# Down projection of an encoder layer: casts of the second token half's first eight tiles in two portions, and the first weight unit of each output pair taken tile by tile

## The reference, cut to what matters

```
def swiglu(x, w_gate, w_up, w_down):
    return (jax.nn.silu(x @ w_gate) * (x @ w_up)) @ w_down
...
    h = h + FFN_RES * swiglu(rmsnorm(h, ffn1_norm[layer]), ffn1_w_gate[layer], ffn1_w_up[layer], ffn1_w_down[layer])
    h = h + token_mixing(...)
    h = h + FFN_RES * swiglu(rmsnorm(h, ffn2_norm[layer]), ffn2_w_gate[layer], ffn2_w_up[layer], ffn2_w_down[layer])
return rmsnorm(h, final_norm)[:, N_META:]
```

## Time and profile before

| | |
|---|---|
| median of 3 runs | 2661.55 us (2661.48 to 2663.52) |
| profiled execution: its own time, its span | 2661.98 us, 2660.0 us |
| mean granted TensorE clock | 0.968 of full speed |
| busy: PE, DVE, ACT, POOL | 2492.4, 1634.8, 754.2, 126.2 us |
| second phase of the first block | about 613 to 935 us |
| second phase of the second block | about 2317 to 2640 us |

### The profile page before, as it was taken

How to read it: one execution, slowest core, us unless ns; L and a number is a source line. 1 busy time by engine, 2 the same in 40 slices (tenths; PEclk the granted TensorE clock), 3 DMA queues, 4 the chain that set the end, 5 groups by cost and what they waited for, 6 DMA issues and landing times.

```text
span 2660.0 us, 37759 instructions
## 1 busy us (share of the span) xinstructions
PE 2492.4 (94%) x15811; PEld 2375.9 (89%) x15811; DVE 1634.8 (61%) x1967; ACT 754.2 (28%) x1005; POOL 126.2 (5%) x233
## 2 busy tenths in 40 slices
PE   5999999999999999898989878959999999999998
PEld 4899999999999988787877757859999999999998
DVE  6766666665142357877878776386666666643422
ACT  6222222223132322232222323152222222322321
POOL 2000000002010000000000000100000000201000
PEclk8999999999999999999999979989999999999999
DMA  5212212217252311011011211311221222454331
GB/s 201 65 56 78 75 57 77 75 49 289 75 177 96 124 44 32 25 34 37 17 42 34 85 55 40 116 36 62 68 78 62 68 78 67 164 184 129 122 107 62
DMA packets 204581, 222.32 MB, mean 84 GB/s; under 512 B 7552, under 2 KB 182336, under 8 KB 204416
## 3 DMA queue, kind: packets, MB, share of 16 engines
q1 hardware_dynamic: 180848, 119.09, 15.1%
q0 software_dynamic: 23568, 100.81, 10.1%
HBM read 165.82 MB, written 54.05 MB: 83 GB/s over the span
## 4 chain that ended last, share of the span: by engine, by line
PE 83%; DVE 10%; issue 3%; ACT 2%; DMA 1%; DVEq 0%; POOL 0%; ACTq 0%; SPq 0%; POOLq 0%
PE PS L641 39%; PE PS L682 23%; PE PS L547 15%; PE PS L733 2%; DVE COUT L1979 1%; DMA WR<-in_ffn_w_down 1%; PE PS L738 1%; DVE BF L1868 1%; DVE BB L1868 0%; PE PS L614 0%; DVE XB L1692 0%; PE PS L765 0%; DVE AB L1866 0%; DVE WL L1404 0%; PE PS L867 0%
## 5 line engine op out<-in xcount | busy, mean ns | idle before, releaser
L641 PE MATMUL PS<-XB,AW 128*128 128x324 f32 (+1 forms) x5280 | 960.9, 312 | 45.7 <-DVE AW L1639 28.0
L641 PEld LDWEIGHTS PS<-XB,AW 128*128 128x128 f32 x5280 | 828.2, 189 | 48.3 <-DVE AW L1639 30.0
L1404 DVE TENSOR_TENSOR WL<-WR,WH 128x1024 fp32r<-128x1024 f32 (+1 forms) x135 | 153.5, 1137 | 416.6 <-ACT WH L1110 377.8
L682 PE MATMUL PS<-XB,WH 128*128 128x324 f32 (+1 forms) x2048 | 389.7, 312 | 14.9 <-DVE H L1700 9.4
L682 PEld LDWEIGHTS PS<-XB,WH 128*128 128x128 f32 x2048 | 326.1, 190 | 16.4 <-DVE H L1700 9.9
L641 PE MATMUL PS<-HR,AW 128*128 128x324 f32 (+1 forms) x1408 | 323.9, 311 | 0.0
L547 PE MATMUL PS<-XH,WH 128*128 128x512 f32 (+2 forms) x864 | 230.6, 376 | 10.8 <-issue 6.0
L641 PEld LDWEIGHTS PS<-HR,AW 128*128 128x128 f32 x1408 | 238.5, 190 | 0.0
L682 PE MATMUL PS<-XB,WL 128*128 128x324 f32 (+1 forms) x1024 | 235.8, 312 | 0.0
L1089 ACT ACTIVATE AW<-AS 128x512 fp32r<-128x512 f32 x176 | 111.3, 632 | 427.8 <-PE PS L641 427.8
L547 PE MATMUL PS<-XL,WH 128*128 128x512 f32 (+2 forms) x864 | 219.8, 363 | 0.0
(11 more groups left out here) (262 smaller groups left out, 2794.9 us busy)
## 6 DMA issues: line engine op xcount, KB each, us to landing
WR<-in_ffn_w_down SPq DMA_DIRECT2D x78, 512.0 KB, 3.5
AR<-in_ffn_w_gate SPq DMA_DIRECT2D x44, 512.0 KB, 3.9
AR<-in_ffn_w_up SPq DMA_DIRECT2D x44, 512.0 KB, 5.2
WR<-in_w_in SPq DMA_DIRECT2D x28, 512.0 KB, 3.8
hidden<-QT POOLq DMA_DIRECT2D x22, 648.0 KB, 3.2
hidden<-QT POOLq DMA_DIRECT2D x22, 640.0 KB, 3.4
XBF<-hidden POOLq DMA_DIRECT2D x32, 324.0 KB, 5.1
XBF<-hidden POOLq DMA_DIRECT2D x32, 320.0 KB, 4.9
```

The source lines that it names most:

```text
L641: mm = nc.tensor.matmul(PAIR[q_ % 3][:, q, 0:qw], w[:, slot, kk * P:(kk + 1) * P], x[:, q * qw:(q + 1) * qw], start=first, stop=kk == KH - ...
L682: mm = nc.tensor.matmul(bank[:, q, 0:qw], wt[:, slot, col:col + P], x[:, q * qw:(q + 1) * qw], start=opens, stop=last and wt is WL)
L1404: tt(WL[:, s, 0:n], WR[:, s, 0:n], WH[:, s, 0:n].bitcast(F32), ALU.subtract).then_inc(split_lo[s], 1)
```

## The change

Two edits. The first swaps the loops within a unit that holds hidden tile 0, which is the first unit of each pair: output tile outside, hidden tile inside, so all four steps of the first output tile come before the four of the second. (Units 42 and 45 also hold hidden tile 0, but have one output tile, and their order stays.) The second edit splits the casts of half 1's first eight hidden tiles: four at unit 22 and four at unit 23, on ACT (first hunk of the two) and on DVE alike. They stay behind the same unit's `split_down`.

```
-DOWN_STEPS = [(u, h, d, f) for u, (h, ds, fs) in enumerate(DOWN_UNITS) for f in fs for d in ds]
+DOWN_STEPS = [(u, h, d, f) for u, (h, ds, fs) in enumerate(DOWN_UNITS)
+              for d, f in ([(d, f) for d in ds for f in fs] if 0 in fs else [(d, f) for f in fs for d in ds])]
...
-                    if u == 22:
-                        nf[0] = 0
-                    if u == 23:
-                        while nf[0] < 8:
+                    if u in (22, 23):
+                        nf[0] = 4 * (u - 22)
+                        while nf[0] < 4 * (u - 21):
                             hidden_high(1, F_ORDER[nf[0]])
                             nf[0] += 1
...
-                    if u == 22:
-                        nf = 0
-                    if u == 23:
-                        while nf < 8:
+                    if u in (22, 23):
+                        nf = 4 * (u - 22)
+                        while nf < 4 * (u - 21):
                             hidden_low(1, F_ORDER[nf])
                             nf += 1
```

## The result

The changed kernel takes 2644.02 us (median of 4 runs, 2643.49 to 2648.18) against 2662.53 us before (4 runs): ratio 0.9934, interval 0.9917 to 0.9951. Three more comparisons of the same two kernels, made beside the experiments, gave 0.9945 (0.9932 to 0.9959), 0.9932 (0.9918 to 0.9946) and 0.9933 (0.9920 to 0.9947). The medians lie 18.5, 15.0, 18.6 and 16.5 us apart. The forecast was 2646.6 and a gain of 15.0.

A forecast was written before the change was run, and what follows sets the result against it. PE was taken to bound the kernel, waiting on the takes at the change of halves; 7.56 + 7.42 = 14.98 us off 2661.98 gave 2647.0, and with the median 0.43 lower, 2646.6 us; range 2643.5 to 2652.0.

The forecast's parts named there:

- The bound: Whole kernel: PE is busy 2492.4 of 2660.0 us, so time it loses in the changed phase is kernel time.
- The casts: Unit 22, each block: four casts and four low parts (3.02 us of DVE) fit idle time, some 3 us spare; cost 0.
- The takes and the fifth step: Unit 24, each block: earlier takes free PE's banks before its fifth step, with 0.71 and 0.67 us to spare.
- What is late next: DVE after the takes: work for unit 26 ends at 779.27, against unit 26 at 785.73; no new wait.
- rival 4: First units: steps into the same PSUM banks are slower, 27.6 us in all, giving 2674.2 us; chance 0.03.
- The sum: Unit 24's place in both blocks: 7.56 + 7.42 = 14.98 us gained, from waiting and slow clock removed.
- the clock elsewhere: Mixer, four heads: granted clock may change by up to 6.3 us either way; taken as 0.
- A sign that came up: Mixer: a change of its span by more than 2 us would show the forecast wrong; it was expected unchanged.
- Rival 1: Unit 24, both blocks: takes still too late, 4.4 us lost, 2651.0 us, or 2656.4 with slow clock; chance 0.07.

## Why the prediction was right

- *The bound.* PE's wait on the take was the loss, and its end came through to the program's end. The removed wait was named with its place, and the wait's length follows the number of low parts ahead of the takes in four kernels (eight, six, four, none: 4.72, 3.23, 1.74 us, no wait).
- *The casts.* Forecast: they fit in idle time with 3 us to spare, `split_down(25)` unmoved. Measured: 2.95 us left on DVE ahead of those weights, which start 2.19 us before unit 24 (768.48 and 770.67); before it was 2.21.
- *The takes and the fifth step.* Forecast: takes 2 us into unit 24 and 0.7 us to spare. Measured: 1.92 us, and no wait in any profile of the changed kernel.
- *What is late next.* Nothing was: the low parts for unit 26 end at 775.21 + 3.06 = 778.27.
- *The same banks, rival 4.* Unit 24 tile by tile takes 7.11 us, as unit 42. In the second block it takes 7.06, 0.03 more than the unit at full clock in the earlier trace rows: next to no price.
- *The sum.* 14.98 forecast, 14.96 in the profile. The time came out 2.6 us under the forecast in the first comparison, since the median moved by 18.5: a term taken as 0 with a bound of 6.3 us, the clock elsewhere, is large enough to hold that, and it is where the profiles of one program differ most. That it was the cause is not shown: the profile of that comparison gained only 13.8 us.
- *Luck in the number.* That term was put at 0 because whole runs of the kernel before lay within 2 us, and the range allowed 3 us for it below the forecast. Those were three runs; in the later comparisons its runs lie 5.8, 9.7 and 6.9 us apart. The measured 2644.02 is only 0.5 us above the lower end of the range, and the 2642.97 of the third comparison is below it. The 15 us in the two units are no luck; that the whole time fell in so narrow a range is in part.
- *A sign that came up.* The prediction held itself wrong if the mixer's span changed by more than 2 us. In the first profile after it was 3.2 us longer, in the three others 0.4 longer, 2.1 shorter and 0.1 shorter. So the sign appeared, but in both directions within one program, and is read here as spread, not as an effect of the change.
- *Where a step was wrong.* Rival 1 was priced on the premise that a wait of 2.2 us costs no slow clock, from the earlier trace rows. In the kernel with the first edit alone one wait of 2.06 us did and one of 2.04 us didn't. Its price was 4.4 us, or 9.8 with slow clock in both blocks; measured were 6.4, between the two.
- *What the prediction didn't see.* It treated the two edits as parts of one gain. All eight casts at unit 22 give the same without the tile order: eight low parts just fill DVE's idle time there, and the takes then stand behind none.

## What to carry to other kernels

When PE waits on an engine that is idle for most of the phase, look at what stands ahead of the awaited instruction in that engine's list: work with slack belongs in an earlier gap, and the list's order is the whole price. Count a PE wait at its length and, from about 2 us on, add what the clock may take behind it; here a wait of 4.9 us cost 7.5. A gain of this size is read from its place in the trace: whole runs of one program here differ by more than the last edits were worth.

## What the runs showed of the hardware

Equal waits of PE are not followed by equal clock. Of the waits looked at, idle times of 1.74, 1.77, 2.04, 2.17 and 2.85 us were followed by full pace; 2.06, 3.23 (twice), 3.28, 4.68 and 4.72 us by matmuls at about half pace, near the lower level of 1.2 GHz (granted 0.54 and 0.59 in the windows shown, the longest of 6.23 us). The 2.04 and the 2.06 come from the same kernel and the same place in its two blocks, and the slow stretch after the latter began 1 us after PE had started again. (The 2.85 is the wait ahead of unit 1 in the kernel with all casts at unit 22, the 2.17 that of the earlier trace rows.) What slow clock took behind the waits of 2.06 and 3.23 us was the same each time, about 1.65 us; behind 4.72 us it was 2.68. The Trainium skill ("TensorE: Matmul & The Clock Gate", section "What's actually happening") says that the watch over PE's activity runs freely, not from the kernel's start; these waits agree with it.
